# The convolution rows of a state-space layer, made in four column quarters of TensorE

## What is computed

```
def s5_mixer(h, w_in, lam_re, lam_im, log_step, b_re, b_im, c_re, c_im, d_skip, w_glu):
    u = (h @ w_in).reshape(bsz, seq, SSM_GROUPS, SSM_GROUP).astype(f32)     # 64 groups of 16
    ...                                                                     # 64 complex states per group
        _, _, xr, xi = lax.associative_scan(combine, (ar_seq, ai_seq, bu_re, bu_im), axis=0)
        return jnp.einsum('gkn,lgn->lgk', cr, xr) - jnp.einsum('gkn,lgn->lgk', ci, xi)
    y = lax.map(scan_sequence, u)
    y = y + d_skip.astype(f32).reshape(SSM_GROUPS, SSM_GROUP) * u
```

## Time and profile before

| what | value |
|---|---|
| median of 3 runs | 1815.95 us (1815.52 to 1817.81) |
| the profiled execution | 1813.56 us |
| its span, first to last instruction | 1811.8 us |
| granted TensorE clock, mean | 0.99 |
| busy PE / DVE / ACT / POOL | 1760.3 / 818.2 / 669.2 / 696.5 us |

### The profile page before, as it was taken

One profiled execution on the slowest core, in us unless ns is written; L12 is line 12 of the kernel. 1 busy time (PEld: TensorE's weight loads), 2 busy tenths in 40 slices (PEclk: granted clock), 3 DMA queues, 4 the chain that ended last, 5 costly groups with the idle time before them and its releaser, 6 DMA issues.

```text
span 1811.8 us, 22254 instructions
## 1 busy us (share of the span) xinstructions
PE 1760.3 (97%) x8782; PEld 1465.3 (81%) x8782; DVE 818.2 (45%) x1446; ACT 669.2 (37%) x1128; POOL 696.5 (38%) x314
## 2 busy tenths in 40 slices
PE   8999999999999898999999999999999999999999
PEld 6887877787788677789888888888888888888887
DVE  4876999679867537414211111147665311111111
ACT  3332334143243555624321322266755333122221
POOL 5422334435434221243453444424711244344442
PEclk9999999999999898999999999999999999999999
DMA  9422324443535446322333333222200333332332
GB/s 239 104 71 82 85 77 144 125 139 117 166 111 164 138 168 212 119 93 82 103 95 93 89 104 98 82 83 74 75 1 14 93 94 93 94 104 85 102 95 80
DMA packets 242279, 189.60 MB, mean 105 GB/s; under 512 B 41472, under 2 KB 199296, under 8 KB 242176
## 3 DMA queue, kind: packets, MB, share of 16 engines
q1 hardware_dynamic: 238176, 180.33, 33.4%
q10 hardware_dynamic: 4000, 7.84, 1.3%
HBM read 168.74 MB, written 19.40 MB: 104 GB/s over the span
## 4 chain that ended last, share of the span: by engine, by line
PE 80%; DVE 14%; ACT 3%; issue 1%; DMA 1%; POOL 0%; DVEq 0%; SPq 0%; ACTq 0%
PE ps L368 11%; PE ps L370 11%; PE ps L369 11%; PE ps L394 9%; PE ps L395 9%; PE ps L396 9%; PE ps L425 3%; PE ps L427 3%; PE ps L426 3%; PE ps L876 2%; PE ps L857 2%; DVE h_b L1910 1%; DVE tmp L1906 1%; PE ps L867 1%; DVE k_s L1934 1%
## 5 line engine op out<-in xcount | busy, mean ns | idle before, releaser
L1002 POOL TENSOR_TENSOR w_lo<-w_raw,w_hi 128x1024 fp32r<-128x1024 f32 (+3 forms) x283 | 668.6, 2373 | 1080.3 <-ACT w_hi L1129 1080.2
L368 PE MATMUL ps<-a_hi,w_hi 128*128 128x512 f32 (+1 forms) x1184 | 442.4, 374 | 4.4 <-POOL w_lo L1002 4.4
L370 PE MATMUL ps<-a_hi,w_lo 128*128 128x512 f32 (+1 forms) x1184 | 440.5, 372 | 0.0
L369 PE MATMUL ps<-a_lo,w_hi 128*128 128x512 f32 (+1 forms) x1184 | 440.3, 372 | 0.0
L1129 ACT ACTIVATE w_hi<-w_raw 128x1024 fp32r<-128x1024 f32 (+3 forms) x283 | 285.0, 1019 | 215.9 <-DMA w_raw<-in_ffn_w_gate_up_dram 71.4
L368 PEld LDWEIGHTS ps<-a_hi,w_hi 128*128 128x128 f32 x1184 | 223.0, 188 | 45.5 <-issue 7.2
L370 PEld LDWEIGHTS ps<-a_hi,w_lo 128*128 128x128 f32 x1184 | 223.0, 188 | 38.8
L369 PEld LDWEIGHTS ps<-a_lo,w_hi 128*128 128x128 f32 x1184 | 223.1, 188 | 38.3
L2118 DVE TENSOR_TENSOR ev<-ps,xh 128x512 f32<-128x512 f32 x44 | 30.4, 692 | 411.9 <-PE ps L370 383.0
L394 PE MATMUL ps<-w_hi,h_hi 128*128 128x512 f32 x476 | 190.5, 400 | 7.1 <-DVE x_rows L1623 3.4
L396 PE MATMUL ps<-w_hi,h_lo 128*128 128x512 f32 x476 | 189.4, 398 | 0.0
(11 more groups left out here) (344 smaller groups left out, 2396.4 us busy)
## 6 DMA issues: line engine op xcount, KB each, us to landing
w_raw<-in_ffn_w_gate_up_dram SPq DMA_DIRECT2D x88, 512.0 KB, 3.8
w_raw<-in_w_up_dram SPq DMA_DIRECT2D x44, 512.0 KB, 3.9
w_raw<-in_ffn_w_down_dram SPq DMA_DIRECT2D x40, 512.0 KB, 3.8
w_raw<-in_w_in_dram SPq DMA_DIRECT2D x20, 512.0 KB, 4.4
w_raw<-in_w_down_dram SPq DMA_DIRECT2D x20, 512.0 KB, 4.3
s_records<-stage SPq DMA_DIRECT2D x16, 544.0 KB, 5.2
w_raw<-in_ssm_w_glu_dram SPq DMA_DIRECT2D x16, 512.0 KB, 3.7
rec<-s_records SPq DMA_DIRECT2D x12, 544.0 KB, 3.8
```

Of the source, the lines that this page charges most:

```text
L368: pe.matmul(bank, wh, xh_, start=first, stop=False)
L369: pe.matmul(bank, wh, xl_, start=False, stop=False)
L370: return pe.matmul(bank, wl, xh_, start=False, stop=last)
L1002: pool.tensor_tensor(w_lo[:, n % RING, 0:w], w_raw[:, n % RING, 0:w], w_hi[:, n % RING, 0:w].bitcast(F), ALU.subtract).then_inc(lo_made, 1)
```

## The change

The four matmuls of a batch write to partitions 0, 32, 64 and 96 of their bank (`KQ * g`), all in columns 0 to 127. `k_s` becomes 128 partitions x 2 x 240: the four groups lie on four quarters of the partitions, and the even and odd batches in two places of the free dimension. ACT copies 128 x 128. d is laid out to match (`d_c`, a column per batch; the 16 unused partitions of each quarter are zeroed by POOL once), next to four copies of the 16 x 16 identity (`d_at`), and the diagonal is one instruction. Since a group now lies on partitions of its own, SP stores each group by itself: 32 DMAs per batch instead of 8.

```
-N_CONST, N_TURNED, N_PARAM = 13, 8, 5
+N_CONST, N_TURNED, N_PARAM = 13, 8, 7
...
-        k_s = scratch("k_s", [KQ + GK, GB, KPAD + P], F, 55)
+        k_s = scratch("k_s", [P, 2, KPAD + P], F, 55)
...
                 for g in range(GB):
-                    m = pe.matmul(b[0:GK, g * P:g * P + P], h_bs[f % 2][:, g, T - 1, :],
+                    m = pe.matmul(b[KQ * g:KQ * g + GK, 0:P], h_bs[f % 2][:, g, T - 1, :],
                                   stages[f % 2][:, P_O + g * 144:P_O + g * 144 + P], start=True, stop=True)
...
-        def k_rows(f):
-
-            return k_s[KQ * (f % 2):KQ * (f % 2) + GK]
+        def k_rows(f, g):
+
+            return k_s[KQ * g:KQ * g + GK, f % 2, :]
...
+            pool.memset(d_c[:, :], 0.0).then_inc(d_zeroed, 1)
...
-                    for o in (0, KQ):
-                        sp.dma_start(d_t[o:o + GK, :], ssm_d_2[0].rearrange("(g k) -> k g", g=G)).then_inc(p_in, 16)
+                    sp.wait_ge(d_zeroed, 1)
+                    for g in range(GB):
+                        sp.dma_start(d_c[KQ * g:KQ * g + GK, :],
+                                     ssm_d_2[0].rearrange("(f g k) -> g k f", g=GB, k=GK)[g]).then_inc(p_in, 16)
...
-                    sp.dma_start(rec_dram[f, GK * s:GK * s + GK, M_O:C_O].rearrange("p (g c) -> p g c", g=GB),
-                                 k_rows(f)[:, :, o:o + P]).then_inc(k_out[f % 2], 16)
+                    for g in range(GB):
+                        sp.dma_start(rec_dram[f, GK * s:GK * s + GK, M_O + g * P:M_O + g * P + P],
+                                     k_rows(f, g)[:, o:o + P]).then_inc(k_out[f % 2], 16)
...
-                b = full(act, ("s5k", f))[0:GK, :].rearrange("p (g c) -> p g c", g=GB)
-                release(("s5k", f), act.activation(k_rows(f)[:, :, KPAD:], b, ACT.Copy))
+                b = full(act, ("s5k", f))[:, 0:P]
+                release(("s5k", f), act.activation(k_s[:, f % 2, KPAD:], b, ACT.Copy))
...
-                at_f = slice(KQ * (f % 2), KQ * (f % 2) + GK)
-                dk = tmp1[at_f, 0:GB * GK].rearrange("p (g c) -> p g c", g=GB)
-                step(v.tensor_tensor(dk, ident[at_f, at_f].unsqueeze(1).to_broadcast([GK, GB, GK]),
-                                     d_t[at_f, f * GB:f * GB + GB].unsqueeze(2).to_broadcast([GK, GB, GK]), ALU.mult))
-                o = k_rows(f)[:, :, KPAD:KPAD + GK]
-                v.tensor_tensor(o, o, dk, ALU.add).then_inc(k_w, 1)
+                o = k_s[:, f % 2, KPAD:KPAD + GK]
+                v.scalar_tensor_tensor(o, d_at[:, :], d_c[:, f:f + 1], o, ALU.mult, ALU.add).then_inc(k_w, 1)
...
             go(v.memset(k_s[:, :, 0:KPAD], 0.0))
+            for g in range(GB):
+                at_g = slice(KQ * g, KQ * g + KQ)
+                go(v.tensor_copy(d_at[at_g, :], ident[at_g, KQ * g:KQ * g + GK]))
```

More of the change, by code:

```diff
@@ L165, in program @@
         lam = scratch("lam", [P, 3, G], F, 86.5)
-        d_t = scratch("d_t", [KQ + GK, G], F, 61.5)
+        d_c = scratch("d_c", [P, NB], F, 61.5)
+        d_at = scratch("d_at", [P, GK], F, 61.5, 4 * NB)
         stages = [scratch("stage0", [P, M_O], F, 41), scratch("stage1", [P, M_O], F, 32)]
@@ L286, in program @@
         k_w = sem("k_w")
+        d_zeroed = sem("d_zeroed")
         rec_state = [sem(f"rec_state{i}") for i in range(RECS)]
@@ L1090, in _ @@
                 sp.wait_ge(st_out[i], 16 * (NB // 2))
-                sp.wait_ge(k_out[i], 16 * (NB // 2) * T)
+                sp.wait_ge(k_out[i], 16 * (NB // 2) * T * GB)
             sp.wait_ge(e_out, 16 * NB)
@@ L1192, in s5_batch_out @@
                 if f >= 2:
-                    act.wait_ge(k_out[f % 2], 16 * T * (f // 2))
-                b = full(act, ("s5k", f))[0:GK, :].rearrange("p (g c) -> p g c", g=GB)
-                release(("s5k", f), act.activation(k_rows(f)[:, :, KPAD:], b, ACT.Copy))
+                    act.wait_ge(k_out[f % 2], 16 * T * GB * (f // 2))
+                b = full(act, ("s5k", f))[:, 0:P]
+                release(("s5k", f), act.activation(k_s[:, f % 2, KPAD:], b, ACT.Copy))
                 if f >= 2:
@@ L1332, in _ @@
                 act.wait_ge(st_out[i], 16 * (NB // 2))
-                act.wait_ge(k_out[i], 16 * (NB // 2) * T)
+                act.wait_ge(k_out[i], 16 * (NB // 2) * T * GB)
             act.wait_ge(e_out, 16 * NB)
```

## The result

The changed kernel takes 1824.87 us (median of 6 runs, 1820.25 to 1827.54), the kernel before 1816.18 us beside it (1815.18 to 1819.11). The ratio is 1.0041, 95% interval 1.0029 to 1.0053: **slower by 8.7 us**, where 8.3 us less were forecast. The profiled execution has 1823.35 us, a span of 1821.5 and a mean clock of 0.986.

The account below looks back on a forecast made before the run. PE, busy 97% of the span, was taken as the bound. Terms -3.0 - 3.6 - 2.5 - 1.4 + 2.2 = -8.3 us, against the shown median of 1815.95, gave 1807.6 us; range 1800 to 1824.

Parts of the forecast that it names:

- The step that failed: SP's stores before batches 8 and 11: claimed that later stage stores and buffer releases keep no one waiting; no time charged.
- The forecast's slower rival: SP becomes the bound through dearer DMAs, with stalls at 496 and 590; about 1824 us, chance 0.22.
- stall at 496: In the slower rival, PE waits for a late weight chunk at 496 behind the bursts of batches 8 and 9.
- SP's bursts: Stores of k_s on SP: 32 DMAs at 0.454 us, 14.5 us per batch instead of 3.6.
- The chunk at 496: Weight chunk behind the stores of batches 8 and 9: ready at 493.8, PE begins it at 496.34; cost 0.
- The stall at 590: Weight chunk behind batch 13's burst, ready at 592.6, wanted by PE at 590.52: +2.2 us, ends 0 and +8.
- -3.0 forecast: PE's matmuls in four column quarters: 0.37 us saved per batch, counted in eight batches; ends 0 and -5.9.
- half way: Overlap of PE's eight passes: five steps of eight, 0.61 us, between no saving and 0.73 us saved.
- DVE's stall and the clock: Near 328: one diagonal operation fewer ends PE's wait for x_rows, -3.6 us, and the half clock behind it, -2.5.
- gain taken over by others: Rival: POOL's operations stretch another DVE operation, x_rows stays late; -3.0 and +2.2 remain, 1815 us, chance 0.20.
- The wait for `stage` at 451.5: PE's wait of 1.3 us there goes as POOL makes chunks later; -1.4 us with restart, ends -2.5 and +1.
- The end: ACT waits for all records before reading them back; batch 15 stores by 623.4, just before; no time charged.

Follow-up runs that it names:

- e1: The changed kernel with 8 merged stores of k_s per batch instead of 32, each carrying four shifts of a group; 1810.59 us, ratio 0.9957.
- e3: The kernel before with its eight stores of k_s per batch split by group into 32, nothing else of the change; 1830.25 us, ratio 1.0075.
- e6: e1 with the four matmuls per batch back in one column quarter, ACT copying four pieces; 1813.64 us, ratio 0.9984.
- e10: The kernel before with 32 stores in batch 2 alone, eight in the others, nothing else of the change; 1812.25 us, ratio 0.9966.
- e8: e1 with 32 stores in batch 2 alone; 1805.78 us, ratio 0.9939.
- e4: The changed kernel with each batch's 32 stores in lots of eight, behind its stage store and the next weight loads; 1824.96 us, ratio 1.0035.
- e5: e4 with the 32 stores of the last batch issued at once; 1824.79 us, ratio 1.0038.
- e11: e8 with four stores per batch (a group's eight shifts in one DMA), batch 2 still with 32; 1805.37 us, ratio 0.9934.
- e7: e1 with the diagonal in two DVE operations instead of one; 1806.31 us, ratio 0.9938.

## Why the prediction was wrong

**The step that failed** is in the part on SP: "The stage buffer that DVE reuses for batch 11 comes free later too, and that falls into a stretch where DVE has time", with "Batch 7 is stored before SP is due for batch 8". Batch 7's burst ends at 449.35, and batch 8's stage store leaves only at 451.40. The one who waits first is batch 10's table product, 10.07 us, with the additions to x_rows behind it: PE waits 8.5 us and loses 10.5 from 440 to 489, the clock behind the stall included. The kernel before already had a wait of 1.0 us at that place. e1, with short bursts, waits 0.7 us there and has no stall; e3, the kernel before with long ones, waits 6.6 us and has one of 5.0. Following each weight load to its chunk and leaving the stage stores, which stand in the same queue, with one sentence was the mistake. The wait of batch 11 (8.09 us, until 477.78) was indeed harmless, as put: PE waits for nothing between 470 and 590.

**The forecast's slower rival** named SP as the bound, and its time, 1824 us, came out. That is luck: it had a DMA at 0.65 us, and at least 0.57 before the gains were used up, but the bursts ran at 0.46 to 0.52. Its stall at 496, which was to cost 10.0 of the 16.3 us, did not come, and the larger loss was at a place that it does not name.

**SP's bursts**: 14.5 us forecast, 14.7 to 16.8 seen; nearly right. **The chunk at 496** holds; right. **The stall at 590**: +2.2 forecast, 3.2 us of wait seen, at the place named. The load took 6.1 us to land where 4.3 was put. With the half clock behind it (0.50 to 600), PE loses 5.5 us to 610. Mis-sized, mostly since no clock was charged to a new stall, though the earlier trace rows had shown what one costs.

**PE**: -3.0 forecast (0.61 us for the eight passes, eight batches). Measured 0.34 us, thus 0.64 saved where 0.37 was taken, and about nine batches pass it on from 352 to 610 (e1 against e6: 5.8 us). The term should have been near -6. The estimate from the Trainium skill ("TensorE: Matmul & The Clock Gate", Part 3), 0.41 us and -4.5, was the nearer of the two. The step "half way" was the weak one, as no row bore on overlap at all.

**DVE's stall and the clock**: -3.6 and -2.5 forecast; 7.4 us gained from 310 to 352. The size was nearly right, by luck, and the reason was wrong. e1 keeps the single operation and has the stall, 5.3 us; e10 and e3 keep both old operations and have none. What removes it in the changed kernel is the long burst of batch 2, which holds POOL off: e8 puts that burst back into e1, and the stall goes. So the term that was to pay for the change was paid by the change's cost, and the rival "gain taken over by others" described the operation rightly.

**The wait for `stage` at 451.5**: -1.4 forecast, but it is there, 1.8 us; wrong. **The end**: batch 15's burst ends at 632.4, not 623.4, and meets no one only because the kernel is late; e4 and e5, which are early, lose nearly 16 us there (with longer runs of stores at the end). The forecast, which had PE early too, gave this place no price.

**The sum.** What the quarters and the paused POOL bring to 440 us is 6.2 us, and 2.6 more come from 489 to 586. The two stretches with stalls in the shadow of SP's bursts take 10.5 and 5.5; 1.6 us go after 610, much as in e8 and e11. That makes +8.8 at 730. From 730 to 1700, where the programs are the same, the kernels drift by another 1 to 4 us against the kernel before, in steps before 760 and between 1200 and 1300; why was not tried.

## What to carry to other kernels

A queue is in order for everything in it: when DMAs are added, list what stands behind them, stores that free a buffer included, and follow each to who waits for it; a store that leaves behind such a burst and the due loads lands later too. In e8, where only batch 2 has a long burst, the stage's store behind it and its four loads takes 9.2 us to land, and 5.2 in e1. That the clump of loads is what slows it is argued, and was not tried by itself. A gain in a trace need not come from the part of the change that was meant to make it: undo the parts one by one, and try the cost alone on the old kernel. Before splitting a transfer by partition groups, see whether one access pattern can carry several shifts of a group: 8 DMAs in place of 32 turned the loss of 8.7 us into a gain of 6.

## What was not expected of the hardware

The issue of a DMA on SP hardly depends on how much it carries: 427 ns (median) for four groups of 16 rows of 128 elements, and 420 for one such group. Merging pays nearly in full. But the DMAs of e1, whose pattern steps back 16 columns in `k_s`, take 595 ns with as many elements as the old ones. With twice as many, in e11, a burst of four takes 2.5 us, the same 0.63 each as e1's eight in 5.0. So it is not the number of pieces that makes them dearer; which property of the pattern does was not tried.

Four matmuls in four column quarters, two passes each, take 0.34 us to the next matmul, less than three steps of 0.12, where the forecast's argument by dependences had left five steps.

Small shifts of POOL decide several microseconds. In e1 POOL starts 0.04 us before DVE's last table operation of batch 3 begins (325.11 and 325.15), in e7 2.3 us after it has begun (326.77 and 324.46). The two programs differ by one operation of 0.2 us per batch, and the one with more operations is 4.3 us faster.
